# Token attention in a new order: values one pair behind, the compressed branch in spare score columns, outputs turned per pair, bias fetched sooner

## The chip, the cores and the metric

One NeuronCore of a Trainium2 chip runs the whole program in one launch. The metric is the device time in microseconds (us), the median of the runs shown. The engines are called by what they are: TensorE (PE in the profile, PEld its weight loads), VectorE (DVE), ScalarE (ACT), GpSimd (POOL) and SyncE (SP, which issues the loads of weight tiles).

## The reference

x is 256 tokens by 1024 features. Four mixers and their feed-forward layers follow each other: latent attention, an mLSTM, a short convolution, and last a token attention with three branches ("nsa"). Only the last matters here. It has 16 heads of 64 in 4 key groups:

```
proj = x @ w_q                                   # 1024 query columns, 48 gate columns
q    = rmsnorm per head(proj[:, :1024])
gate = sigmoid(proj[:, 1024:])                   # (head, branch)
s_c  = q @ k_c.T / 8 + bias                      # 15 compressed keys
o_c  = softmax(s_c) @ v_c                        # zero for the first 31 tokens
s_s  = q @ k_s.T / 8 + bias; o_s = softmax(s_s) @ v_s     # all 256 keys, causal
s_w  = q @ k_w.T / 8 + bias; o_w = softmax(s_w) @ v_w     # all 256 keys, causal
out  = (gate0 * o_c + gate1 * o_s + gate2 * o_w) @ w_o
```

With 256 tokens both the selected and the window branch see every earlier key, so a head has two score matrices of the same shape and the same bias, with other keys and values. The bias depends on the distance between query and key through 32 buckets.

## The kernel before

**Weights.** 522 tiles of 128 x 1024 float32 stream through four slots (`raw`). SyncE loads a slot when the tile before it has been split. ScalarE copies the tile to a rounded form (`split`, L502 to L510, `w_hi`), VectorE takes the rest (`take_lo`, L960, `w_lo`), GpSimd does this (L446) for tiles in three stretches, the last of them the tiles loaded during the query projection. A product is three matmuls of rounded operands, so most of the program is TensorE fed by this stream. Order on each engine is the order of the text; engines meet through counting semaphores.

**Around the change.** `residual("out_2")` is the second half of the feed-forward layer before: 8 outputs of 3 tiles each. After it ScalarE issues eight DMAs (L936 to L941), 256 KB each, which lay the bias of every head out by query and key (`bias`, from `bias_dram`). `bias` shares its memory with `os`, which the feed-forward layer read.

`nsa` on TensorE (L1961) first projects the gates (one tile) and the queries (`token_major("nq")`, 8 tiles, 16 chunks, two halves of 8 heads). Pieces of the attention stand between chunks: turning the queries of the first half (L1964) after chunk 9, compressed scores (L1975) after 11, turning the compressed probabilities (L1986) after 13, compressed values (L1993) after 15. Compressed scores need the turned queries, which ScalarE copies out (L822) after squares, root and two splits. Then the second half of the compressed branch is done, and then the head loop:

- TensorE `scores` (L2005, L2006): per head and branch, 128 queries against 128 keys and 128 against 256. The operand is a copy of the head's queries with zeros in the other 64 rows, made by ScalarE (`queries`, L845).
- VectorE `logits` (L1507): scores times the query's norm plus bias, two instructions for both branches; `maxima` (L1515 to L1517): maximum per query and branch, negated.
- ScalarE `exps` (L853): four exponentials with accumulated sums.
- VectorE `scales` (L1522, L1526): gate over sum. GpSimd (L496) multiplies the probabilities by it.
- TensorE `turn_probs` (L2019): six 128 x 128 turns; ScalarE copies them (L861).
- TensorE `values` (L2034): both branches accumulate into one output; VectorE adds it to the compressed output (`outputs`, L1535).

Logits run two heads ahead, and the buffers of logits and probabilities are two each. After the last head the outputs are turned (L1804), split by ScalarE and VectorE into `os` (L694, L1158), and the output projection `residual_one("wo_n")` begins, with the other turns between its first chunks.

Of the kernel before, what the change touches and what calls it, by code (L numbers as in the profile page):

```python
# [27 lines left out]
ALU = mybir.AluOpType  # L28
# [108 lines left out]
def build(nc, x_in, tiles, vecs, rows, consts, rel_bias, w1c_k, w1c_v, w2c_k, w2c_v, y_out):  # L137
    ctx = ExitStack()
    with ctx:
# [31 lines left out]
        vtok = sb("vtok", [P, TB * 2 * G * DH])  # L171
        kcT = sb("kcT", [P, G * NC])
        vc = sb("vc", [G * NC, G * DH])

        with nc.sbuf_tensor("os", [P, KD * 2 * S], F32R) as os_:
            pass
# [16 lines left out]
        def const(name, a, z, p=slice(None)):  # L193
# [39 lines left out]
        n_gturn, n_sqd, n_sum, n_std_, n_turn, n_qTd, n_cs, n_clog, n_cexp, n_cT, n_cTs, n_cpv, n_co = (  # L233
            sem(f"n_{n}") for n in ("gturn", "sqd", "sum", "std", "turn", "qTd", "cs", "clog", "cexp", "cT", "cTs", "cpv", "co"))
        n_gs, n_pg = sem("n_gs"), sem("n_pg")
        n_zero = sem("n_zero")
        n_q, n_s, n_log, n_max, n_exp, n_pT, n_pTd, n_pv, n_od = (
            sem(f"n_{n}") for n in ("q", "s", "log", "max", "exp", "pT", "pTd", "pv", "od"))
# [128 lines left out]
        n_qT = [[part(14720 + S * (2 * j + e), S) for e in range(2)] for j in range(2)]  # L367
        n_l = [part(8896 + 768 * j, 768) for j in range(2)]
        n_p = [part(10432 + 768 * j, 768) for j in range(2)]
        n_pTs = [part(11968 + 768 * j, 768) for j in range(2)]  # L370
        n_mx, n_nmx, n_rs, n_sc = ([part(13504 + 16 * j + 4 * w, 4) for w in range(4)] for j in range(4))
        n_cl = [part(13568 + H * NC * tb, H * NC) for tb in range(TB)]
        n_cmx, n_crs, n_csc = (part(14048 + TB * H * j, TB * H) for j in range(3))
        n_cpT = arena[0:G * NC, 14144:14144 + 2 * S]
# [22 lines left out]
        SQ0 = {"mix_0": 0, "cq": KD} | {name: KD + 1 + KD * j for j, name in enumerate(RES)}  # L397

# [40 lines left out]
        def _(pool):  # L439
# [49 lines left out]
            for t in range(*POOL_TILES[2]):  # L489
                take_lo(t % RING, t)  # L490
            with pool.Fori(0, HG) as i:
                for w in range(4):
                    pool.wait_ge(n_gs, i * 4 + (w + 1))
                    for tb, (a, z) in enumerate([(0, P), (P, 3 * P)]):
                        probs = n_p[w % 2].rearrange("p (b c) -> p b c", b=2)[:, :, a:z]
                        ins = pool.tensor_tensor(probs, probs, n_sc[w][:, 2 * tb:2 * tb + 2].unsqueeze(2).to_broadcast([P, 2, z - a]), ALU.mult)  # L496
                    ins.then_inc(n_pg, 1)
# [3 lines left out]
        def _(act):  # L501
# [41 lines left out]
            def residual(name, per, outs=KD):  # L543
# [19 lines left out]
                if last:  # L563
                    for i in range(outs // 4):
                        four(i)
                else:
                    act.preload_act_table(ACT.Sqrt)
                    with act.Fori(0, outs // 4) as i:
                        four(i)
# [120 lines left out]
            def out_hi(name, chunks=range(KD), gain=None):  # L690

                for k in chunks:
                    act.wait_ge(o_turn[name], k + 1)
                    act.activation(hi_part(os_, k), bank(5 + k % 3, 0, S), ACT.Copy,  # L694
# [97 lines left out]
            def nsa():  # L792
# [3 lines left out]
                split(t0 + RING)  # L796
                act.wait_ge(n_zero, 1)
                act.wait_ge(n_gturn, 1)
                for tb in range(TB):
                    ins = act.activation(n_gate[:, tb * 3 * H:(tb + 1) * 3 * H], bank(7, tb * 3 * H, (tb + 1) * 3 * H), ACT.Sigmoid,  # L800
                                         scale=rstd[:, tb:tb + 1])
                ins.then_inc(n_gates, 1)
                for t in range(t0 + 1, t0 + 4):
                    split(t + RING)

                def squares(g):
                    act.wait_ge(out_read, OUT0["nq"] + 2 * g + 2)
                    if g:
                        act.wait_ge(n_sum, 2)
                    for tb in range(TB):  # L810
# [71 lines left out]
                def four(i):  # L882

                    last = isinstance(i, int) and i == HG - 1
                    for w in range(4):
                        if w % 2 == 0 and not last:
                            queries(i + 1, w // 2)
# [1321 lines left out]
```

## Time and profile before

| what | us |
|---|---|
| median of 3 runs | 1666.72 (1665.49 to 1666.77) |
| the profiled run, its own time | 1666.71 |
| its span | 1664.9 |
| TensorE busy | 1602.7 |
| VectorE, ScalarE, GpSimd busy | 1099.6, 885.4, 163.7 |
| first matmul of the query projection | 1334.39 |
| first matmul of the output projection | 1452.53 |

Times inside the profile count from the start of the span. A row of a timeline gives the start, the duration, the engine, the line and the shapes, xN where N alike instructions are merged, and in brackets how long the engine was idle before it and what ended the wait. A matmul's duration includes its way through the array, so the next one starts before it ends: the distance of starts is what it costs. A float32 matmul appears as two instructions.

### The profile page before, as it was taken

Reading aid. Unit: us, or ns where it says so; the run is one execution under the profiler, and the core shown is the slowest. Engines: PE = TensorE matmul, PEld = TensorE weight load, DVE = VectorE, ACT = ScalarE, POOL = GpSimd, SP = SyncE. Lnnn points to the kernel's source line nnn. Section 1 sums busy time; section 2 is a strip of 40 time slices with the busy share of each in tenths; the row PEclk is TensorE's granted clock in tenths of the full one; section 3 lists DMA queues with packets and bytes.
Section 4 is the critical chain, followed back from the end, with each engine's and each line's share of the span. In section 5 each row is a group of like instructions: output and inputs, shape, how many; then the busy total and the mean of one; then the engine's idle time right before and its main releaser. Section 6 shows DMA issues by size and latency. Waiting matters only on the chain.

```text
span 1664.9 us, 33598 instructions
## 1 busy us (share of the span) xinstructions
PE 1602.7 (96%) x11652; PEld 1510.1 (91%) x11652; DVE 1099.6 (66%) x1770; ACT 885.4 (53%) x1468; POOL 163.7 (10%) x141
## 2 busy tenths in 40 slices
PE   7899999999999999999999999997999988799999
PEld 7789998977999899998999999897999867799997
DVE  6667766544876667667877666785566728676665
ACT  5676554535655445455446445544545546664443
POOL 1640000266000000000000000000000053300000
PEclk9999999989999999999999999998999989999999
DMA  6136566544566556556655555656455680055564
GB/s 228 64 82 199 188 190 190 176 131 135 178 190 188 191 176 198 182 187 203 191 188 189 190 188 187 206 182 196 145 189 186 210 171 15 1 175 186 184 197 142
DMA packets 81246, 282.81 MB, mean 170 GB/s; under 512 B 8848, under 2 KB 12432, under 8 KB 81168
## 3 DMA queue, kind: packets, MB, share of 16 engines
q1 hardware_dynamic: 77376, 276.88, 52.4%
q10 hardware_dynamic: 3792, 4.85, 1.7%
q8 instruction: 54, 0.88, 0.2%
q14 instruction: 24, 0.20, 0.0%
HBM read 280.12 MB, written 1.57 MB: 169 GB/s over the span
## 4 chain that ended last, share of the span: by engine, by line
PE 88%; DVE 5%; ACT 3%; issue 2%; DMA 1%; ACTq 1%; POOL 0%; DVEq 0%; SPq 0%; POOLq 0%
PE psum L1651 17%; PE psum L1653 17%; PE psum L1652 17%; PE psum L1643 17%; PE psum L1644 9%; PE psum L1779 2%; PE psum L1780 2%; PE psum L1781 2%; ACT arena L853 1%; DMA raw<-tiles 1%; DVE w_lo L968 1%; PE psum L2034 1%; PE psum L1941 1%; DVE arena L1517 0%; DVE arena L1516 0%
## 5 line engine op out<-in xcount | busy, mean ns | idle before, releaser
L510 ACT ACTIVATE w_hi<-raw 128x1024 fp32r<-128x1024 f32 x522 | 550.5, 1056 | 462.8 <-PE psum L1653 266.3
L968 DVE TENSOR_TENSOR w_lo<-raw,w_hi 128x1024 fp32r<-128x1024 f32 x476 | 582.0, 1223 | 229.0 <-ACT w_hi L510 228.2
L1651 PE MATMUL psum<-xs,w_hi 128*128 128x256 f32 x1960 | 550.7, 281 | 6.1 <-DVE w_lo L968 5.0
L1653 PE MATMUL psum<-xs,w_lo 128*128 128x256 f32 x1960 | 549.8, 280 | 0.0
L1652 PE MATMUL psum<-xs,w_hi 128*128 128x256 f32 x1960 | 547.9, 280 | 0.0
L1643 PE MATMUL psum<-hs,w_hi 128*128 128x512 f32 x1216 | 421.9, 390 | 0.0
L1651 PEld LDWEIGHTS psum<-xs,w_hi 128*128 128x128 f32 x1960 | 369.6, 189 | 7.2 <-DVE w_lo L968 5.5
L1652 PEld LDWEIGHTS psum<-xs,w_hi 128*128 128x128 f32 x1960 | 369.7, 189 | 0.2
L1653 PEld LDWEIGHTS psum<-xs,w_lo 128*128 128x128 f32 x1960 | 369.2, 188 | 0.0
L1644 PE MATMUL psum<-hs,w_lo 128*128 128x256 f32 x1216 | 343.4, 282 | 0.0
L1643 PEld LDWEIGHTS psum<-hs,w_hi 128*128 128x128 f32 x1216 | 228.3, 188 | 47.1
L448 POOL TENSOR_TENSOR w_lo<-raw,w_hi 128x1024 fp32r<-128x1024 f32 x46 | 110.3, 2411 | 1228.1 <-ACT w_hi L510 1198.0
L1644 PEld LDWEIGHTS psum<-hs,w_lo 128*128 128x128 f32 x1216 | 230.5, 190 | 0.0
L1651 PE MATMUL psum<-os,w_hi 128*128 128x256 f32 x544 | 154.5, 284 | 1.6 <-DVE os L1158 1.6
L1652 PE MATMUL psum<-os,w_hi 128*128 128x256 f32 x544 | 152.7, 281 | 0.0
L1653 PE MATMUL psum<-os,w_lo 128*128 128x256 f32 x544 | 152.6, 281 | 0.0
L1651 PEld LDWEIGHTS psum<-os,w_hi 128*128 128x128 f32 x544 | 103.2, 190 | 2.5 <-DVE os L1158 2.4
L1652 PEld LDWEIGHTS psum<-os,w_hi 128*128 128x128 f32 x544 | 103.2, 190 | 0.0
L1653 PEld LDWEIGHTS psum<-os,w_lo 128*128 128x128 f32 x544 | 103.1, 189 | 0.0
L991 DVE SCALAR_TENSOR_TENSOR xs<-x,vec,xs 128x256 fp32r<-128x256 f32 (+1 forms) x80 | 38.1, 482 | 51.7 <-ACT xs L524 51.7
L524 ACT ACTIVATE xs<-x,vec (+1 forms) x80 | 40.2, 509 | 54.3 <-DVE x L1058 31.2
L1106 DVE TENSOR_TENSOR fsum<-psum,sil 128x256 f32<-128x256 f32 x88 | 37.4, 425 | 46.0 <-PE psum L1653 44.7
(282 smaller groups left out, 1643.8 us busy)
## 6 DMA issues: line engine op xcount, KB each, us to landing
raw<-tiles SPq DMA_DIRECT2D x522, 512.0 KB, 4.2
bias<-bias_dram ACTq DMA_DIRECT2D x8, 256.0 KB, 12.5
x<-x_in SPq DMA_DIRECT2D x4, 256.0 KB, 5.7
y_out<-x SPq DMA_DIRECT2D x8, 128.0 KB, 3.5
con<-consts SPq DMA_DIRECT2D x1, 771.0 KB, 9.2
bias_dram<-bias_row ACTq DMA_DIRECT2D x1, 512.0 KB, 7.2
row<-rows SPq DMA_DIRECT2D x1, 192.0 KB, 9.2
vec<-vecs SPq DMA_DIRECT2D x1, 80.5 KB, 1.9
```

Of the source, the lines that this page charges most:

```text
L448: pool.tensor_tensor(w_lo[s][:, :], raw[s][:, :], w_hi[s][:, :].bitcast(F32), ALU.subtract).then_inc(lo_ready, 1)
L510: act.activation(w_hi[s][:, :], raw[s][:, :], ACT.Copy).then_inc(hi_ready, 1)
L524: act.activation(dst, src, ACT.Copy, scale=gain).then_inc(xhi_ready, 1)
L968: dve.tensor_tensor(w_lo[s][:, :], raw[s][:, :], hi_of(w_hi[s][:, :]), ALU.subtract).then_inc(lo_ready, 1)
L991: dve.scalar_tensor_tensor(out=dst, in0=src, scalar=gain, in1=hi_of(hi), op0=ALU.mult, op1=ALU.subtract).then_inc(xs_ready, 1)
L1106: dve.tensor_tensor(f, bank(b, 0, S), sil[u // 2][:, :] if u % 2 else rb[:, :], ALU.mult).then_inc(out_read, 1)
L1643: pe.matmul(bank(out_bank), w_hi[s][:, c:c + P], src[:, chunk:chunk + 2 * S], start=first, stop=False)
L1644: return pe.matmul(bank(out_bank, 0, S), w_lo[s][:, c:c + P], src[:, chunk:chunk + S], start=False, stop=last)
L1651: pe.matmul(out, w_hi[s][:, c:c + P], x_hi, start=first, stop=False)
L1652: pe.matmul(out, w_hi[s][:, c:c + P], x_lo, start=False, stop=False)
L1653: return pe.matmul(out, w_lo[s][:, c:c + P], x_hi, start=False, stop=last)
L1779: pe.matmul(out, x_hi, w_hi[s][:, col:col + 512], start=c == 0, stop=False)
```

## The change

- **Bias.** `residual("out_2")` is given `between=bias_rows` on ScalarE: DMA number g goes out after output g. The bias row is stored negated.
- **Queries.** They are evacuated with minus 1/8 of the norm's factor, normalised per head by VectorE before the turn, and the turn of the first half stands after chunk 13. Scores are thus negated logits, and minima take the place of maxima. `n_l` has four buffers, in the memory of `xs`.
- **Gates.** Sigmoid is computed as 1 / (1 + exp(-x)), beside the other exponentials.
- **Scores.** For a pair of heads at once, straight from the turned queries: head 0 of the pair in rows 0 to 63, head 1 in rows 64 to 127, alternately.
- **Logits.** `tensor_tensor_reduce`: bias added and the minimum taken in one instruction, four per head.
- **Values.** `vtok` has a column of ones per head, so the row sums come with the values. Branches have separate columns; VectorE scales them by gate over sum, GpSimd adds them and the compressed output. Values run one pair behind the turns.
- **Compressed branch.** Its scores, turns and values use columns 384 to 511 of the score banks, one step per pair, ahead of the pair's scores.
- **Outputs.** Output chunk k is turned when pair k is complete (`n_oo`), chunks 0 and 1 before the last turn of probabilities; banks by `out_bank`.
- All loops over heads are written out.

```diff
+            def bias_rows(g):
+                act.dma_start(bias[g * COPIES:(g + 1) * COPIES, :].rearrange("p (h s) -> p h s", h=H),
...
+            residual("out_2", FF2_TILES, between=bias_rows)
...
                 squares(0)
+                roots(0)
                 split(t0 + 4 + RING)
-                roots(0)
                 queries_turned(0)
                 split(t0 + 5 + RING)
+                squares(1)
+                roots(1)
+                act.preload_act_table(ACT.Exp)
+                exps(0, 0)
+                gates()
                 compressed_exps(0)
                 exps(0, 1)
+                for k in range(PAIRS):
+                    if k == 2:
+                        queries_turned(1)
+                    probs_turned(k, 0)
+                    if k + 1 < PAIRS:
+                        exps(k + 1, 0)
+                    probs_turned(k, 1)
+                    if k == 3:
+                        compressed_exps(1)
+                    if k + 1 < PAIRS:
+                        exps(k + 1, 1)
+                    if k < 2:
+                        split(t0 + 6 + k + RING)
...
+                def logits(k, e):
+                    h = 2 * k + e
+                    dve.wait_ge(n_s, h + 1)
+                    if k >= 2:
+                        dve.wait_ge(n_exp, h - 3)
                     for tb, (a, z) in enumerate([(0, P), (P, 3 * P)]):
+                        table = bias[:, h * S + (P if tb == 0 else 0):(h + 1) * S]
+                        for br in range(2):
+                            m = 2 * tb + br
+                            ins = dve.tensor_tensor_reduce(out=n_l[h % 4][:, br * 384 + a:br * 384 + z], in0=bank(n_bank[2 * e + br], a, z), in1=table,
+                                                           scale=1.0, scalar=3.0e38, op0=ALU.add, op1=ALU.min,
+                                                           accum_out=n_mn[h % 4][:, m:m + 1])
+                def outputs(k, e):
+                    dve.wait_ge(n_pv, h + 1)
+                    then(dve.reciprocal(ri.unsqueeze(2), pv[:, :, DH:DH + 1]))
+                    then(dve.tensor_tensor(sc..., ri..., gate4[:, :, h, 1:3], ALU.mult))
+                    dve.tensor_tensor(n_br[h % 4]..., pv[:, :, 0:DH], sc..., ALU.mult).then_inc(n_od, 1)
...
+                for k in range(PAIRS):                       # VectorE
+                    if k + 1 < PAIRS:
+                        logits(k + 1, 0)
+                        dve.wait_ge(n_s, 2 * k + 4)
+                        g, step = divmod(k + 1, 4)
+                        if step == 0:
+                            compressed_logits(g)
+                        if step == 1:
+                            compressed_turned(g)
+                        if step >= 2:
+                            compressed_outputs(g, step - 2)
+                    if k:
+                        outputs(k - 1, 0)
+                    if k + 1 < PAIRS:
+                        logits(k + 1, 1)
+                    if k:
+                        outputs(k - 1, 1)
+                    if k % 4 == 0:
+                        compressed_scales(k // 4)
...
+                def scores(k):                               # TensorE
+                    if k == PAIRS // 2:
+                        pe.wait_ge(n_qTd, 4)
+                    pe.wait_ge(n_log, 2 * k)
+                    g, step = divmod(k, 4)
+                    if step == 0:
+                        compressed_scores(g)
+                    if step == 1:
+                        compressed_turn(g)
+                    if step >= 2:
+                        compressed_values(g, step - 2)
+                    for block in BLOCKS:
+                        for e in range(2):
+                            ins = score(k, e, *block)
...
+                warm(12, 6)
+                for k in range(PAIRS):
+                    if k == 0:
+                        turn_probs(0, 0)
+                    if k + 1 < PAIRS:
+                        scores(k + 1)
+                    if k == 2:
+                        turn_queries(1)
+                        values(1, 0)
+                    if k:
+                        turn_probs(k, 0)
+                    if k not in (0, 2):
+                        values(k - 1, 0)
+                    if k == PAIRS - 1:
+                        pe.wait_ge(n_log, H)
+                        turn_outputs("o_n", no_tok, (n_oo, 1), range(2))
+                    if k == 2:
+                        values(1, 1)
+                    turn_probs(k, 1)
+                    if k not in (0, 2):
+                        values(k - 1, 1)
+                values(PAIRS - 1, 0)
+                values(PAIRS - 1, 1)
+                turn_outputs("o_n", no_tok, (n_oo, 1), range(2, 4))
```

## Rows read from the trace of the kernel before

**Rows 1.** The page: its first line, and from the list of DMA issues the weight tiles.

```profile
span 1664.9 us, 33598 instructions
...
raw<-tiles SPq DMA_DIRECT2D x522, 512.0 KB, 4.2
```

**Rows 2.** Busy time by stretches, start:end, length, then each engine; last clock, DMA share, GB/s.

```profile
1262.00:1331.00 69.00, 69.00 (x423) 62.15 (x422) 48.51 (x69) 37.96 (x53) 0.00 (x0) 1.00 0.63 199
1334.40:1352.80 18.40, 18.35 (x84) 14.38 (x83) 3.46 (x10) 6.25 (x9) 9.55 (x4) 1.00 1.11 173
1358.80:1372.30 13.50, 13.48 (x52) 11.12 (x52) 4.17 (x15) 7.08 (x13) 5.33 (x3) 0.71 0.31 95
1372.30:1388.40 16.10, 13.12 (x75) 11.00 (x75) 12.80 (x37) 11.17 (x31) 3.40 (x3) 0.89 0.18 63
1388.40:1451.00 62.60, 49.59 (x378) 46.01 (x378) 45.28 (x113) 42.35 (x153) 24.15 (x30) 1.00 0.00 1
```

**Rows 3.** Timeline of ScalarE at the start of the stage.

```profile
1331.76 4.11 ACTq L939 DMA_DIRECT2D bias<-bias_dram  x7
...
1352.61 1.06 ACT L510 ACTIVATE w_hi<-raw 128x1024 fp32r<-128x1024 f32 x1 [5.35 <-DMA raw<-tiles]
```

**Rows 4.** Timeline of TensorE in and after the query projection.

```profile
1336.57 0.40 PE L1779 MATMUL psum<-w_hi,xs 128*128 128x512 f32 x1
1336.81 0.40 PE L1780 MATMUL psum<-w_lo,xs 128*128 128x512 f32 x1
...
1358.82 3.62 PE L1975 MATMUL psum<-kcT,arena 128*128 128x30 f32 x16 [6.06 <-ACT arena L822]
...
1375.89 1.87 PE L1975 MATMUL psum<-kcT,arena 128*128 128x30 f32 x16
```

**Rows 5.** Timeline of TensorE in the head loop, and the output projection's first matmul.

```profile
1391.78 0.39 PE L2005 MATMUL psum<-kT,arena 128*128 128x128 f32 x2
...
1393.09 1.50 PE L2034 MATMUL psum<-vtok,arena 128*128 128x128 f32 x12
1394.43 0.82 PE L2019 MATMUL psum<-con,arena 128*128 128x128 f32 x6
...
1452.53 0.39 PE L1651 MATMUL psum<-os,w_hi 128*128 128x256 f32 x1 [0.50 <-DVE os L1158]
```

**Rows 6.** Timeline of VectorE between the projection and the head loop.

```profile
1370.60 1.41 DVE L1441 TENSOR_SCALAR arena<-psum,rstd 128x512 f32<-128x512 f32 x2 [4.55 <-PE psum L1781]
...
1377.31 0.17 DVE L1517 TENSOR_SCALAR arena<-arena 128x4 f32<-128x4 f32 x1
...
1377.88 0.41 DVE L1464 TENSOR_TENSOR arena<-psum,arena 128x56 f32<-128x56 f32 x2
...
1379.31 0.41 DVE L1476 TENSOR_TENSOR arena<-arena 128x56 f32<-128x56 f32 x2
```

**Rows 7.** Timeline of VectorE in the head loop.

```profile
1427.37 1.13 DVE L1507 SCALAR_TENSOR_TENSOR arena<-psum,arena,bias 128x256 f32<-128x256 f32 x2
...
1430.64 0.76 DVE L1517 TENSOR_SCALAR arena<-arena 128x4 f32<-128x4 f32 x1
...
1431.51 1.13 DVE L1507 SCALAR_TENSOR_TENSOR arena<-psum,arena,bias 128x256 f32<-128x256 f32 x2
```

**Rows 8.** Timeline of ScalarE in the head loop, one head.

```profile
1427.29 0.40 ACT L853 ACTIVATE arena<-arena 128x128 f32<-128x128 f32 x1 [1.44 <-DVE arena L1517]
1427.60 0.19 ACT L853 ACTIVATION_READ_ACCUMULATOR arena<-arena 128x1 f32 x1
...
1429.06 0.84 ACT L845 ACTIVATE arena<-arena 64x256 f32 x2
```

**Rows 9.** Timeline of GpSimd in the head loop.

```profile
1429.77 1.61 POOL L496 TENSOR_TENSOR arena<-arena 128x256 f32<-128x256 f32 x2 [2.54 <-DVE arena L1526]
```

**Rows 10.** DMA queues in 1325:1400, the queue of the bias; packets, MB, share.

```profile
q10 hardware_dynamic: 2176, 2.10, 20.6%
```

**Rows 11.** Timeline of ScalarE in the residual stage before.

```profile
1296.36 1.06 ACT L510 ACTIVATE w_hi<-raw 128x1024 fp32r<-128x1024 f32 x1 [1.59 <-PE psum L1644]
```

More of the change, by code:

```diff
@@ L541, in residual_one, with residual @@
                         split(t0 + u + RING, i)
-            def residual(name, per, outs=KD):
+            def residual(name, per, outs=KD, between=None):
                 t0, o0 = TILE0[name], OUT0[name]
@@ L882, in four @@
[L882 to L887, printed above, removed]
-                        probs_turned(i, w)
-                        if not (last and w >= 2):
-                            exps(i if w < 2 else i + 1, (w + 2) % 4)
-                four(0)
-                with act.Fori(1, HG - 1) as i:
-                    four(i)
@@ L1555, in nsa @@
+                logits(0, 1)
+                gates()
                 query_scales(1)
-                compressed_logits(1)
-                logits(0, 1)
-                maxima(0, 1)
-                compressed_scales(1)
-                scales(0, 0)
-                compressed_outputs(1)
-                dve.wait_ge(n_co, 2)
-                def four(i):
-                    first, last = (isinstance(i, int) and i == j for j in (0, HG - 1))
-                    for w in range(4):
-                        two_on = (i if w < 2 else i + 1, (w + 2) % 4)
-                        if not (last and w >= 2):
-                            logits(*two_on)
-                        if not (last and w == 3):
-                            scales(i if w < 3 else i + 1, (w + 1) % 4)
-                        if not (last and w >= 2):
-                            maxima(*two_on)
-                        if not (first and w == 0):
-                            outputs(i if w else i - 1, (w - 1) % 4)
@@ L1590, in _ @@
+                out_lo("o_n", range(2))
+                outputs(PAIRS - 1, 0)
+                outputs(PAIRS - 1, 1)
+                out_lo("o_n", range(2, KD))
             dve.wait_ge(vec_loaded, 16)
@@ L2048, in nsa @@
-                compressed_turn(1)
-                scores(0, 2)
-                compressed_values(1)
-                def four(i):
-                    first, last = (isinstance(i, int) and i == j for j in (0, HG - 1))
-                    for w in range(4):
-                        if not (last and w >= 1):
-                            scores(i if w < 1 else i + 1, (w + 3) % 4)
-                        if not (first and w == 0):
-                            values(i if w else i - 1, (w - 1) % 4)
-                        turn_probs(i, w)
@@ L2062, in nsa @@
[L2062 to L2067 removed]
+                                                  13: lambda: turn_queries(0)})
+                pe.wait_ge(n_qTd, 2)
+                for block in BLOCKS:
+                    ins = score(0, 0, *block)
+                ins.then_inc(n_s, 1)
+                pe.wait_ge(out_read, OUT0["nq"] + 4)
```

402 lines of the change are left out of this document (182 added, 220 removed).

## The prediction

> **What bounds the kernel now.** I read the page first, then the busy table by stretches, then the timelines of each engine inside the stretch that the change touches, since that is where a gap has an owner. In the weight-streaming stages TensorE has no gap: in 1262:1331 it is busy all 69 us at granted clock 1.00 while the DMA engines are 0.63 busy [rows 2]. The change leaves those stages as they are. It touches the token attention, from the query projection (first matmul at 1334.4, the start of its stretch in [rows 2]) to the first matmul of the output projection at 1452.53 [rows 5]: 118.1 us. There are three parts.
>
> First, the projection. One 512-column matmul starts 0.24 us after the last [rows 4]; 16 chunks of 6 matmuls, a gate turn of 0.4 and a query turn of 0.9 are 24 us, yet the stretch at the lower clock, which holds the last five chunks, reaches to 1372.3 [rows 2], and the second evacuation, which needs only the last chunk, starts at 1370.60 [rows 6]. TensorE stands 6.06 us before L1975 [rows 4]: that matmul waits for the turned queries, ScalarE copies them late, and ScalarE stood 5.35 us for a weight tile [rows 3]. The tile was late because ScalarE had issued seven bias DMAs from 1331.76 [rows 3] whose queue took 20.6% of 16 engines over 75 us, 15.5 us in all [rows 10]. After the gap the clock is down: 0.71 in 1358.8:1372.3 [rows 2].
>
> Second, 1372.3 to 1388.4: compressed branch of groups 8 to 15, between VectorE, ScalarE and TensorE by turns, clock 0.89 [rows 2].
>
> Third, the head loop, 1388.4 to 1451, TensorE busy 49.6 of 62.6 [rows 2]. One head is 4.15 us (from the start of L1507 at 1427.37 to its next at 1431.51, [rows 7]). No engine fills it; it is a ring: exponentials with their four accumulator reads, 1.77 us from 1427.29 to 1429.06 [rows 8], then the reciprocal, the gate product, two maxima and their negation on VectorE up to 1431.4 (L1517's end, [rows 7]), then the next exponentials. L1517 alone is 0.76 us for 4 columns, against 0.17 outside the loop [rows 6, 7]; in the loop it starts at 1430.64 under the POOL product that runs from 1429.77 for 1.61 [rows 7, 9], and it ends when that does. The Trainium skill has a rule for this (SBUF — State Buffer, Who interferes with whom, and the section before it on the two sides): whichever of GpSimd and a VectorE instruction in a two-port mode starts first keeps the pair, and the other "fully blocks". The trace agrees (0.76 against 0.17). By it the 0.6 us goes with L1517, and the new PSUM-reading instructions are not exposed.
>
> **The change, part by part.**
> *Bias fetched in the residual stage before.* The eight DMAs go out one per output of 7.6 us, behind the squares on ScalarE. Each takes 15.5/8 = 1.9 us of all engines, 0.25 of an output; with the 0.63 there [rows 2] that is 0.88. Cover: ScalarE splits a tile at 1296.36 [rows 11], VectorE has its rest 2.3 us later (two instructions of 1.06 and 1.2), and the slot is wanted again four tiles on, 4/3 of an output, 10.1 us; less 2.3, less 4.2 for the load [rows 1] leaves 3.6 us against 1.9. ScalarE pays 8 x 0.6 us of issue (4.11 for seven, [rows 3]) where it is 55% busy [rows 2]. I cost it at nothing; uncovered it is 8 x 1.9 = 15 us. The issues that stood before the norm's root vanish too, but nothing on TensorE's path waited for them.
> *Projection.* Queries are normalised before the turn, the turn moves to chunk 13, compressed scores, turns and values leave the projection. The chain to the turned queries starts with the first half, ready at 1334.4 + 11.6 = 1346.0: evacuation (two 512-column instructions, 1.4 by twice L1507's larger half), squares 0.6 after it, sums 0.7, root 0.3, reciprocal 0.3, two products 1.3: 1350.6, my estimate; the turn stands at 1354.3, so it is covered by over 3 us, and by 1 us if the short steps are double. Weight tiles: slots come free one per two chunks, 2.8 us, and each load is 4.2 us on four slots, so it is ready unless something else holds the queue. TensorE then ends the projection at 1334.4 + 16 x 6 x 0.234 + 1.3 = 1358.1, against 1370.5.
> *Start of attention.* In order from 1358.1: scores of head 0 1.3 (1391.78 to 1393.09 is one head, [rows 5]); second evacuation, until 1359.6; 8 compressed scores 1.9 [rows 4]; scores of head 1 1.3: 1362.9. VectorE: compressed logits 1.8 (from 1377.88 to the end of L1476 near 1379.7, [rows 6]), logits of head 1, 1.4: 1366.2. TensorE: the added 12 warm matmuls (2.6 us) lie under this, until 1365.5. Compressed turn 0.5, scores of pair 1 (1.9, below): 1368.7.
> *Scores from a pair of heads on row halves.* Now 1.31 us a head, 2.6 a pair. After, the same columns, but each matmul uses 64 rows and neighbours use different halves. No row shows two at once. Ends: 1.3 (all overlap) and 3.0 (none, and 0.2 lost at either end). The nearest row is L1975, 16 passes with 30 columns in 1.87 us [rows 4]: there the weight loads set the pace, and a pair's scores have 16 too. I take 1.9. Beside this, the Trainium skill says (TensorEngine Tiling (Array Packing), sections Key Properties and Theoretical Speedup) that 64-row tiles give up to 2x, but that a change of tiling mode drains TensorE, here twice per pair. By the first S would be 1.3; by the second alone, above 2.6. Both ends are in my range from the rows.
> *Logits fused with the minimum.* L1507 (2 instructions, 1.13, [rows 7]), the two maxima L1515 and L1516 and L1517 become 4 instructions of 128 or 256 columns. Low end: the L1507 time, 1.1. High end: L1507 plus both maxima, 2.1 (the maxima fill 1429.6 to 1430.64 before L1517). Four instructions instead of two add about 2 x 0.15; I take L = 1.4 a head, and ScalarE's accumulator reads (0.19 each, half of it beside the next exponential, [rows 8]) go.
> *Outputs.* Row sums come with the values (a ones column), so there is reciprocal 0.2, gate product 0.2 and a 256-column product 0.4: 0.8 a head, instead of L1535's 0.3 and POOL's 1.61 on probabilities [rows 9]. POOL's adds are off the path until the end.
> *The ring after.* Scores of pair k+2 reuse the banks of pair k+1, so they wait for both its logits. From the end of scores: TensorE turns probabilities 0.66 (L2019's 0.82 less the pipelined tail) and takes values 1.34 (1393.09 to 1394.43, [rows 5]), 2.1 with the hand-over; outputs 0.8; logits 1.4; hand-over 0.1; scores 1.9. One pair is 6.3 us. Other bounds: TensorE 1.9 + 2 x 2.0 = 5.9; VectorE 2 x 2.2 = 4.4; ScalarE, now busy 42.4 us for 16 heads [rows 2] or 5.3 for two, loses the reads and the query copies: 4.5. Now two heads take 8.3.
> *Compressed branch inside.* On the ring: four blocks of value matmuls 0.9 each, compressed scores 1.9, turn 0.5, second query turn 0.9 less slack 0.2, compressed logits 1.8 less the 0.5 wait it fills, scales 0.7 of their 1.1: 8.7. The rest fills the 0.6 us in which VectorE waits for values.
> *End.* From the end of the last scores TensorE has turns and values: 4 turns 2.6, 6 values 8.1, four output turns 0.9: 11.6 us, all others inside. The last adds of POOL (0.5 + 0.8) end near +13.5; its chunk is wanted at +15.
> *Sum.* 1368.7, first interval 5.4 (two logits 2.8, the turned compressed weights 0.6, hand-over, scores 1.9; no outputs yet), 5 x 6.3 = 31.5, 8.7, 11.6: 1425.9. In the first interval TensorE idles 2.8 us; after such a gap the clock fell (0.89 in 1372.3:1388.4, [rows 2]): +1.5. First output matmul at 1427.4 against 1452.5: 25 us less. The profiled run took 1666.71, and its span 1664.9 [rows 1]; the median shown is 1666.72, so nothing is to be shifted: **1641.7**.
>
> **Rivals.**
> (a) Row halves overlap fully, S = 1.3: ring 5.7 a pair, 7 x 0.6 less: 1637. For it: different banks and rows; against: the weight loads.
> (b) No overlap with drains, S = 3.0, or the fused instruction at its high end 2.1: ring 7.1 to 7.4; 7 x 0.8 to 1.1 more: 1647 to 1649. Both together 1655.
> (c) The bias DMAs are not covered: up to 15 more, 1657. Against: the 3.6 us above; the loads waited once in [rows 3] only with all eight at once.
> (d) Slower: TensorE's clock falls to 1.2 GHz and stays there through the loop, since it now waits in each pair and half its rows rest in the scores. Then TensorE is the bound, 2 x 5.9 = 11.8 us a pair: 7 x 5.5 = 38, and 9 more in the compressed parts and the end: 1689. It decides from a ring over 9.9 us a pair. Against: 1.00 in the present loop at 79% busy [rows 2], where the new one is above 90%.
> (e) The change does little, as the loop's ring is replaced by an equal one: only the start gains, 12 us: 1655.
>
> **How the numbers follow.** Mine 0.50, (a) 0.13, (b) 0.21, (c) 0.04, (d) 0.04, (e) 0.08. My case alone is 1637 to 1646 (each hand-over of 0.1 could be 0.2, two a pair, and the clock term 0 to 3). The range that leaves out 2 in 10 goes from 1633 to 1656. A difference under 0.2% (3.3 us) could not be told from none. Faster: all but (d) and a tail, 0.94; within 0.2%: 0.02; slower 0.04.
>
> **What would show it.** Right: no gap of TensorE in the projection, its last matmul near 1358; no DMA wait of ScalarE in the residual stage; scores of a pair in 1.9 us; pair to pair 6.3 us without the compressed branch; four fused instructions in 1.4 us; clock 1.00 in the loop; first output matmul near 1427. Wrong: half clock there, a gap of TensorE in the residual stage, or turned probabilities waiting for exponentials instead of scores for logits.

## The result, and the profile after

The changed kernel takes 1636.34 us (median of 1635.40, 1635.66, 1637.02 and 1637.50), the kernel before 1666.11 (1662.73 to 1666.77, four runs): 29.8 us less, ratio 0.983, 95% interval 0.981 to 0.984. Run again later, unchanged, it took 1636.40 (ratio 0.982 [0.980, 0.985]). Forecast were 1641.7 and 25 us less, with 1633 to 1656 as the range. The profiled execution took 1635.4.

The page: first line, TensorE's share, and the two kinds of DMA, against [rows 1] and [rows 10].

```profile
span 1633.4 us, 33428 instructions
...
PE 1593.6 (98%) x11692; PEld 1501.7 (92%) x11692; DVE 1082.1 (66%) x1822; ACT 866.6 (53%) x1380; POOL 151.3 (9%) x133
...
raw<-tiles SPq DMA_DIRECT2D x522, 512.0 KB, 4.3
bias<-bias_dram ACTq DMA_DIRECT2D x8, 256.0 KB, 6.1
```

Busy time by stretches, with the columns of [rows 2]: the projection, the matmuls on ones, the 8 us around the second pair, two pairs of the loop.

```profile
1331.07:1354.98 23.91, 23.91 (x109) 18.90 (x108) 5.82 (x14) 9.79 (x13) 15.43 (x7) 1.00 0.52 157
...
1360.00:1364.40 4.40, 4.40 (x26) 4.33 (x26) 4.04 (x18) 3.33 (x11) 0.00 (x0) 0.64 0.01 2
...
1367.90:1376.00 8.10, 5.93 (x40) 5.24 (x41) 4.61 (x27) 5.75 (x15) 2.35 (x1) 0.79 0.00 0
...
1394.40:1409.70 15.30, 15.21 (x138) 13.38 (x136) 10.45 (x52) 10.03 (x27) 5.04 (x9) 1.00 0.01 2
```

The gap of [rows 4] is gone: TensorE is busy all 23.91 us of the projection. In two pairs of the loop it idles 0.1 of 15.3 us, where it idled 13 of 62.6 before.

Timeline of TensorE, from the projection's last matmul to the second pair, then one pair of the loop and the output projection's first matmul (start, duration, idle time before in brackets). L1999 is the scores, L1993 the compressed values, L2101 the matmuls on ones, L2032 the turn of the probabilities, L2048 the values.

```profile
1354.65 0.40 PE L1783 MATMUL psum<-w_hi,xs 128*128 128x512 f32 x1
1354.98 1.57 PE L1999 MATMUL psum<-kT,arena 64*128 64x128 f32 x8
...
1360.08 4.41 PE L2101 MATMUL psum<-ones 128*128 128x128 f32 x24
1364.32 0.82 PE L2032 MATMUL psum<-con,arena 128*128 128x128 f32 x6
...
1365.51 1.58 PE L1999 MATMUL psum<-kT,arena 64*128 64x128 f32 x16
1367.02 0.88 PE L2032 MATMUL psum<-con,arena 128*128 128x128 f32 x6
1370.07 2.08 PE L1993 MATMUL psum<-vc,arena 128*128 128x128 f32 x8 [2.17 <-DVE arena L1531]
1372.08 2.22 PE L1999 MATMUL psum<-kT,arena 64*128 64x128 f32 x16
...
1401.35 1.58 PE L1999 MATMUL psum<-kT,arena 64*128 64x128 f32 x16
1402.86 0.87 PE L2032 MATMUL psum<-con,arena 128*128 128x128 f32 x6
1403.57 1.50 PE L2048 MATMUL psum<-vtok,arena 128*128 128x128 f32 x12
1404.91 0.82 PE L2032 MATMUL psum<-con,arena 128*128 128x128 f32 x6
1405.57 1.50 PE L2048 MATMUL psum<-vtok,arena 128*128 128x128 f32 x12
1407.11 1.16 PE L1993 MATMUL psum<-vc,arena 128*128 128x128 f32 x8
1408.20 0.49 PE L1999 MATMUL psum<-kT,arena 64*128 64x128 f32 x4
...
1421.22 0.37 PE L1653 MATMUL psum<-os,w_hi 128*128 128x256 f32 x1
```

VectorE in the same pair: the first of the first head's four fused instructions (L1531, adds and minimum), the compressed outputs (L1517), the first of the three instructions of outputs (L1542 to L1547), the first and third of the second head's four. It answers to [rows 7]. `w1c_all` is the memory of `xs`, in which the logits now lie.

```profile
1403.06 0.29 DVE L1531 CUSTOM_DVE_ANT_0 w1c_all<-psum,bias 128x128 f32<-128x128 f32 x1 [0.54 <-PE psum L1999]
...
1404.17 0.69 DVE L1517 TENSOR_TENSOR w1c_all<-psum,arena 128x512 f32<-128x512 f32 x1
1405.11 0.18 DVE L1542 RECIPROCAL arena<-psum 128x4 f32<-128x4 f32 x1 [0.25 <-PE psum L2048]
...
1405.87 0.28 DVE L1531 CUSTOM_DVE_ANT_0 w1c_all<-psum,bias 128x128 f32<-128x128 f32 x1
...
1406.63 0.42 DVE L1531 CUSTOM_DVE_ANT_0 w1c_all<-psum,bias 128x256 f32<-128x256 f32 x1
```

Read together they are the ring. From the end of the scores at 1402.86: turn 0.71, values 1.34 (start to start), hand-over 0.20, outputs 0.76 (1405.11 to 1405.87), the second head's logits 1.18 to 1407.05, hand-over 0.06, compressed values 1.09, scores 1.51: 6.85 a pair, 5.76 without the compressed values. TensorE's own work in a pair is 0.71 + 1.34 + 0.65 + 1.34 + 1.51 = 5.55 and 1.09: 0.2 us less than the ring. The profile shows no idle time for it, but 1405.57 to 1407.11 is 1.54 us where one head's values take 1.34: the wait is there. So two bounds lie 0.2 apart, and an engine that is busy 15.21 of 15.30 us is still not quite the one that sets the pace.

**Where the 31.5 us between the two spans are.** The stage, from the projection's first to the output projection's first matmul, took 118.1 us before [rows 2, 5] and takes 1421.22 - 1331.07 = 90.15: 28.0 less. Behind it the two are equal (212.4 and 212.2). Another 3.3 us are ahead of it, where the change touches nothing but the bias DMAs in the residual stage; e11 is about them.

### The profile page after: what moved, and what is told of

Read it like the earlier page. It is cut to its first block, busy times and chain, and to the rows that moved or that the text cites. A ratio compares the mean times of both kernels' runs of the same rounds, so it can differ in the third digit from the quotient of the medians.

```text
span 1633.4 us, 33428 instructions
## 1 busy us (share of the span) xinstructions
PE 1593.6 (98%) x11692; PEld 1501.7 (92%) x11692; DVE 1082.1 (66%) x1822; ACT 866.6 (53%) x1380; POOL 151.3 (9%) x133
## 4 chain that ended last, share of the span: by engine, by line
PE 92%; DVE 4%; ACT 2%; issue 1%; ACTq 1%; DMA 0%; DVEq 0%; SPq 0%
PE psum L1653 18%; PE psum L1655 18%; PE psum L1654 18%; PE psum L1645 17%; PE psum L1646 9%; PE psum L1781 2%; PE psum L1782 2%; PE psum L1783 2%; PE psum L2048 1%; PE psum L1999 1%; DVE w_lo L979 1%; PE psum L2032 1%; PE psum L1947 1%; PE psum L1852 0%; PE psum L1845 0%
## 5 line engine op out<-in xcount | busy, mean ns | idle before, releaser
L458 POOL TENSOR_TENSOR w_lo<-raw,w_hi 128x1024 fp32r<-128x1024 f32 x46 | 110.8, 2420 | 1232.3 <-ACT w_hi L534 1202.1
```

What stands on the lines that cost most here:

```text
L458: pool.tensor_tensor(w_lo[s][:, :], raw[s][:, :], w_hi[s][:, :].bitcast(F32), ALU.subtract).then_inc(lo_ready, 1)
```

## The experiments

From each trace three marks are used: the projection's first matmul, the first scores, and the output projection's first matmul. "Ones" is the time from the first matmul on ones to the first turn.

| kernel | median us | ratio to before [95%] | projection begins | to first scores | ones | first scores to output projection |
|---|---|---|---|---|---|---|
| changed | 1636.34 | 0.983 [0.981, 0.984] | 1331.07 | 23.91 | 4.24 | 66.24 |
| e12, changed again | 1636.40 | 0.982 [0.980, 0.985] | 1333.67 | 25.45 | 2.78 | 63.18 |
| e2, bias late | 1637.53 | 0.984 [0.981, 0.987] | 1332.19 | 26.79 | 2.78 | 63.18 |
| e3, scores by head | 1643.29 | 0.986 [0.983, 0.990] | 1333.81 | 23.91 | 4.42 | 73.61 |
| e4, no ones | 1636.46 | 0.983 [0.979, 0.986] | 1332.51 | 25.43 | - | 63.38 |
| e5, logits split | 1650.04 | 0.991 [0.990, 0.993] | 1332.49 | 23.92 | 4.38 | 78.48 |
| e6, values same pair | 1645.97 | 0.989 [0.986, 0.991] | 1330.70 | 23.89 | 4.22 | 76.09 |
| e7, values 65 | 1633.37 | 0.982 [0.980, 0.984] | 1331.03 | 23.91 | 2.78 | 62.84 |
| e8, weights later | 1628.51 | 0.977 [0.975, 0.979] | 1323.86 | 25.32 | 4.41 | 66.34 |
| e9, together | 1626.50 | 0.977 [0.974, 0.980] | 1324.30 | 23.89 | 1.13 | 64.32 |
| e10, values forward | 1636.48 | 0.982 [0.980, 0.984] | 1337.05 | 23.90 | 2.79 | 63.52 |

Single runs of one kernel differ by 2 to 6 us, so an effect under some 2 us is read from the marks and not from a median. Each row's marks come from one profiled execution.

**e12: the changed kernel again.** No edit.

> The changed kernel once more, unchanged, on the chip of the last runs. Expected: 1636 us within 2; the projection's first matmul between 1330.7 and 1333.8 us as in the runs so far, the stage from there to the first output matmul 87 to 91 us, by whether the granted clock falls in the matmuls on ones (4.2 to 4.4 us) or not (2.8 us).

Its last two columns are the reason for repeating: the same code takes 66.24 us in one execution and 63.18 in another. The matmuls on ones, in the same place with the same neighbours (the granted clock is the third number from the end):

```profile
1364.09:1366.87 2.78, 2.78 (x25) 2.78 (x25) 2.56 (x16) 2.03 (x8) 0.00 (x0) 1.00 0.01 3
```

At 1.00 they take 2.78 us, at 0.64 in the stretch shown above 4.24; the first 8 us behind them lose another 1.6 (compressed values 2.0 for 1.09, scores 2.15 for 1.51). It fell in five of the nine profiled executions that hold the 12 matmuls on ones, and what chooses them is not known. The same happens at the start of the projection: in e1, e4, e8 and e12 about 3 of its first us are at half clock, and the column "to first scores" has 25.3 to 25.5 for 23.9 in the last three; in the ten other traces the clock stays up there, although TensorE's waits just ahead (0.8 and 0.85 us) are the same in e12 and in the changed kernel's first execution. In e12:

```profile
1334.70:1337.50 2.80, 2.80 (x8) 2.12 (x8) 1.15 (x5) 0.35 (x1) 2.31 (x1) 0.50 0.79 158
```

Comparisons below are therefore made within one kind: 66.2 with low clock there, 63.2 without.

**e1: the bias fetch alone, on the kernel before.**

```diff
-            residual("out_2", FF2_TILES)
-            act.wait_ge(bias_out, 16)
-            act.wait_ge(tile_done, TILE0["out_2"])
-            for g in range(P // COPIES):
-                act.dma_start(bias[g * COPIES:...], ...)
+            residual("out_2", FF2_TILES, between=bias_rows)   # one DMA behind each output
```

> The kernel before with one part of the change alone: the 8 bias DMAs are issued one by one inside out_2. Theory (as in the forecast): the projection loses its gap and lasts 23.9 us from its first matmul as in the changed kernel, not 36; the loop behind it is the old one, so of the change's 29.8 us about 11 to 13 come, 1653 to 1656 us. Rival: the start of the old loop waits for something else (its zero fills, its queries' copies), and only the 6.1 us of TensorE's gap come: about 1660 us.

Measured 1654.44 against 1665.80, ratio 0.994 [0.992, 0.996]: 11.4 us, within the theory's 11 to 13. In its trace the 6.06 us in front of the compressed scores are gone. The stage there is 110.8 us, 7.4 less than before, or 8.9 without the 1.5 us that its first 24 projection matmuls took longer at the lower clock (7.3 for 5.8). The projection did not come down to the theory's 23.9 us: it takes 28.6, since the compressed scores and turns still stand inside it.

**e2: the changed kernel with the bias fetched late.** The same edit backwards.

> The changed kernel with this one part undone: the bias DMAs are issued behind out_2 again. Theory: the projection is again 12 us longer and everything behind it is moved by that, the ring stays at 6.86 us with and 5.8 us without compressed values: 1647 to 1650 us. Rival: part of the longer projection is hidden by the new order, in which logits need the bias first: 1641 to 1644 us.

Both were wrong: 1637.53, no difference that can be told. The weight tile is late again, 18.1 us behind the projection's first matmul against 18.2 in [rows 3] (timeline of ScalarE, the wait in brackets), but TensorE stands only 2.69 us.

```profile
1350.27 1.06 ACT L534 ACTIVATE w_hi<-raw 128x1024 fp32r<-128x1024 f32 x1 [7.82 <-DMA raw<-tiles]
```

The query turn on TensorE, behind it:

```profile
1355.17 1.09 PE L1969 MATMUL psum<-con,arena 128*128 128x128 f32 x8 [2.69 <-DVE arena L1477]
```

The projection is 2.9 us longer (26.79 against 23.91), and that is all. In the kernel before, the compressed branch stood inside the projection and needed the turned queries half way; now only the query turn does, at chunk 13. Issued late, the same 8 DMAs cost 9 to 11 us in the old order and 3 in the new one, by the marks; the medians of e2 and the changed kernel do not separate the 3.

**e3: scores head by head.**

```diff
-                    for block in BLOCKS:
-                        for e in range(2):
+                    for e in range(2):
+                        for block in BLOCKS:
                             ins = score(k, e, *block)
```

> The changed kernel with a pair's 16 score matmuls issued head by head, not in turns of the two halves of the array's rows. Theory A (TensorE binds the loop): the 16 take about 2.6 us as before the change, not 1.51, in each of 7 pairs, and nothing hides it: +7 to +8 us, 1643 to 1645 us. Theory B (the chain logits, exps, turn binds as I forecast): the first head's scores are now ready as early as before or earlier (1.3 us of 2.6), its logits start at once, and less than half of it shows: +0 to +3 us.

7.0 us slower by the medians. The 8 matmuls (16 instructions) take 2.27 us (next row 1412.22) instead of 1.51, and the pair 7.61 (from 1402.34) instead of 6.86:

```profile
1402.34 2.34 PE L1999 MATMUL psum<-kT,arena 64*128 64x128 f32 x16
...
1409.95 2.34 PE L1999 MATMUL psum<-kT,arena 64*128 64x128 f32 x16
1412.22 0.87 PE L2032 MATMUL psum<-con,arena 128*128 128x128 f32 x6
```

Taking turns between row halves saves 0.76 us, all of it on the path: 7 x 0.76 = 5.3, and 2 more where the clock stayed low for longer. It does not separate A from B: the ring holds the whole of the scores, since the turn is queued behind them on TensorE. My B had the path through the first head's logits, which was wrong.

**e4: no matmuls on ones.** `warm(12, 6)` is left out.

> The changed kernel without the 12 matmuls on ones ahead of the first turn of probabilities. In the changed kernel they ran from 1360.08 to 1364.32 us, the first head's exponentials were done at 1361.02. Theory A (they stand in the way): the first turn starts at about 1361.1 and the stage gets 2 to 3.3 us shorter, 1633 to 1634.5 us. Theory B (they hold the clock): without them the granted clock of the next 10 us falls to half, the scores of pair 1 take 3 us and not 1.5, and the stage gets 1 to 4 us longer, 1637 to 1640 us.

No change in the time (1636.46). Both theories hold a half. The turn starts 6.1 us after the first scores instead of 9.3 (7.8 in e12), and then runs at half clock:

```profile
1364.05 1.39 PE L2032 MATMUL psum<-con,arena 128*128 128x128 f32 x6 [1.05 <-ACT arena L869]
...
1366.57 2.10 PE L1999 MATMUL psum<-kT,arena 64*128 64x128 f32 x16
```

The rest of the stage is 63.38 us, e12's 63.18. So the clock can fall with the ones or without them; with 12 of them they stand in the way. One trace without them doesn't tell how often it falls there.

**e5: the fused logits parted.**

```diff
-    ins = dve.tensor_tensor_reduce(out=..., in0=bank(...), in1=table, op0=ALU.add, op1=ALU.min, accum_out=...)
+    ins = dve.tensor_tensor(..., bank(...), table, ALU.add)
...
+    then(ins)
+    for tb, (a, z) in enumerate([(0, P), (P, 3 * P)]):
+        ins = dve.tensor_reduce(n_mn[h % 4][:, 2 * tb:2 * tb + 2], log[:, :, a:z], AX_X, ALU.min)
```

> The changed kernel with each head's four fused add-and-minimum instructions (1.11 us) parted into four adds and two minimum reductions with a wait between, about 2.3 us by the changed kernel's 0.28 and 0.42 us and the old reductions. Theory A (TensorE binds, VectorE idles 1.5 to 3.4 us in each pair): 2.4 us more VectorE work in a pair uses up that idle time and shows with at most 1 us a pair, the stage gets 1 to 7 us longer: 1637 to 1643 us. Theory B (the forecast's chain through VectorE binds): each head's 1.2 us stands in the chain, 2.4 us in each of 7 pairs: +17 us, 1653 us.

13.7 us slower: more than A, less than B. A pair takes 8.46 us (1410.99 to 1419.45), 1.6 more:

```profile
1410.99 1.16 PE L1994 MATMUL psum<-vc,arena 128*128 128x128 f32 x8 [1.57 <-DVE arena L1534]
...
1419.45 1.16 PE L1994 MATMUL psum<-vc,arena 128*128 128x128 f32 x8 [1.65 <-DVE arena L1534]
```

VectorE, from the end of the scores near 1405.2 to 1410.9:

```profile
1405.30 1.15 DVE L1530 TENSOR_TENSOR w1c_all<-psum,bias 128x128 f32<-128x128 f32 x4 [1.48 <-PE psum L2000]
1406.49 1.01 DVE L1534 TENSOR_REDUCE arena<-w1c_all 128x2 f32<-128x256 f32 x2
...
1408.75 1.14 DVE L1530 TENSOR_TENSOR w1c_all<-psum,bias 128x128 f32<-128x128 f32 x4
1409.93 1.01 DVE L1534 TENSOR_REDUCE arena<-w1c_all 128x2 f32<-128x256 f32 x2
```

A head's logits cost 2.12 instead of 1.11. The ring of the changed kernel holds only the second head's, so it would be 7.9; but now VectorE's own row (logits 2.12, a compressed step 0.59, outputs 0.74, logits 2.11) with scores, compressed values and 0.2 of hand-overs is 8.4, and has become the ring. Of VectorE's idle time in the changed kernel only the wait for values in front of the first head's L1542 was spare room (0.25 us in the pair above, 0.25 to 0.57 in the others that have one); the rest is its wait for scores, which comes back in every pair. That VectorE took over rests on this sum (8.4 against 8.46 measured); no further run varies it.

**e6: values behind their own pair.** The order within pair k becomes scores of k+1, both turns of k, both values of k.

> The changed kernel with the values of a pair issued behind the same pair's turns, not one pair behind. Theory: TensorE waits in each pair for ScalarE's copies of the turned probabilities (0.87 us for a head, behind the 1.5 us of the next exponentials), 1.5 to 3 us a pair that nothing else fills: the ring goes from 5.8 to 7.3 to 8.8 us, +10 to +20 us, 1647 to 1657 us. Rival (the order of the values is worth little, the gain is the fused logits and the shorter scores): under 4 us.

9.6 us slower, just under the theory's range: a pair takes 8.66 us. TensorE waits for ScalarE's copies before the second turn, and for VectorE's outputs before each of the values:

```profile
1409.50 1.58 PE L1999 MATMUL psum<-kT,arena 64*128 64x128 f32 x16
...
1412.29 0.85 PE L2032 MATMUL psum<-con,arena 128*128 128x128 f32 x6 [0.40 <-ACT arena L879]
1413.90 1.58 PE L2048 MATMUL psum<-vtok,arena 128*128 128x128 f32 x12 [0.76 <-DVE arena L1547]
1415.76 1.58 PE L2048 MATMUL psum<-vtok,arena 128*128 128x128 f32 x12 [0.28 <-DVE arena L1547]
```

**e7: 65 columns in the values.** `vtok[:, first_v:first_v + DH + 1]` for `first_v + P`.

> The changed kernel with 65 columns in each matmul of values and not 128 (the 63 columns behind a head's values and its ones are not used). Theory A (they are bound by their columns): 1.34 us a head become 0.7 us, 8 us less in 16 heads, and since TensorE binds, 5 to 8 us less: 1629 to 1631 us. Theory B (they are bound by the loads of 128x128 weights, one behind each matmul): the same 1.34 us, 1636 us.

B, nearly: half the columns take 0.05 us less of 1.34 a head, so the columns do not set the pace. That the loads of the weights do fits the trace: they are busy in all 1.29 us of these values, and the compressed scores, with 30 columns and weights as large, take 0.113 us an instruction (16 in 1.80) against 0.112 here with 128 and 0.107 with 65. The row of one head (the next starts 1.29 after it):

```profile
1400.37 1.45 PE L2048 MATMUL psum<-vtok,arena 128*128 128x65 f32 x12
```

The median's 3 us are not from this: 62.84 stands against 63.18 of the changed kernel at the same clock.

**e10: values half a pair sooner.** In pair k now turn of the first head, values of the second head of k-1, turn of the second head, values of the first head of k.

> The changed kernel with one new order alone: the values of a pair's first head are issued behind the same pair's second turn (the first pair's into the idle time of 2.2 us ahead of the second pair's scores), the second head's behind the next pair's first turn. Theory A (TensorE binds the ring): no pair gets shorter, the 1.34 us taken into the idle time are all there is: the stage 1.3 us shorter, and with a clock that stays up there 2 to 3 us, median 1633 to 1635.5 us. Theory B (the chain through VectorE binds): nothing, or 1 to 3 us longer, since outputs stand ahead of the next logits sooner.

Nothing gained (1636.48; 63.52 against 63.18), theory B. The idle time of 2.17 us is filled with values and reappears: 0.84 in the same place, 1.47 one pair later, released by the same logits.

```profile
1374.46 1.16 PE L1993 MATMUL psum<-vc,arena 128*128 128x128 f32 x8 [0.84 <-DVE arena L1531]
...
1381.40 1.16 PE L1993 MATMUL psum<-vc,arena 128*128 128x128 f32 x8 [1.47 <-DVE arena L1531]
```

**e8 and e11: the compression's weights.** A stage before the change's, ScalarE issues four DMAs in a row. The second of them, timeline of ScalarE's queue, in the kernel before:

```profile
1124.97 5.30 ACTq L769 DMA_DIRECT2D w1c_all<-w1c_v  x1
```

The same of the changed kernel:

```profile
1124.30 3.06 ACTq L796 DMA_DIRECT2D w1c_all<-w1c_v  x1
```

Code and place are the same, the issues are not: 5.30 and 3.06 us, and the third takes 4.8 in both. ScalarE does nothing else meanwhile, the keys' root comes behind, and TensorE waits for the keys: 8.7 us before, 6.5 after. All eleven traces without the edit below fall in two kinds: 3.0 to 3.4 us and a wait of 6.5 to 6.7 in eight, 4.7 to 5.3 us and 7.9 to 8.7 in three (before, e10, and e12, which is the changed kernel itself). Both experiments put the DMAs behind that root:

```diff
-            glu("glu_2", {0: key_roots, 9: compressed_hidden, ...})
+            glu("glu_2", {0: key_roots, 1: lambda: hidden_weights(0), 2: lambda: hidden_weights(1),
+                          3: output_weights, 9: compressed_hidden, ...})
```

> The changed kernel with the DMAs of the compression's weights issued inside glu_2, behind the root of the key norms, one at a time, and not ahead of it. In the changed kernel ScalarE stood 8.5 us in their issue (1122.9 to 1132.7) and TensorE then idled 6.5 us for the keys. Theory: that gap goes, 4 to 7 us less: 1629 to 1632 us; and since both kernels' times differ from run to run by how long that issue takes (4.4 to 5.3 us for the first two), the spread gets smaller. Rival: the compression then waits for its weights, and the time stays within 2 us.

> The kernel before with the compression's weights fetched inside glu_2, as in e8. It tells whether the part of the difference that lies ahead of the stage (3.3 us between the two profiled executions) belongs to the change. Theory (it does not: it is how long the issue of those DMAs happened to take): the gain is that of e8, 7 to 8 us, 1657 to 1659 us, and the projection then begins at the same time in both kernels within 1 us (1326 us). Rival: the two kernels still differ there by about 3 us.

e8 takes 1628.51, 7.8 less than the changed kernel where 4 to 7 were expected; its runs did not lie closer together (1622.86 to 1629.76, the changed kernel's 1635.40 to 1637.50). TensorE's only wait in 1100:1180 is 0.6 us (line, released by, total, times, longest):

```profile
PE psum L1951 <- DMA arena<-w2c_v: 0.6, 1, 0.6
```

e11, on the kernel before, takes 1657.00 against 1665.24, 8.2 less, ratio 0.995 [0.993, 0.996], and its five runs lie within 2 us. The projection begins at 1324.33 in e11 and at 1323.86 and 1324.30 in e8 and e9 (not at 1326, as I had expected): old and new within 0.5 us. So the 3.3 us ahead of the stage are not the change's; 2.2 of them are the kind of that issue. The changed kernel's own two traces begin the projection 2.6 us apart. With the issue moved out of both, new against old is e8 against e11: 1628.51 against 1657.00, 28.5 us, from two rounds in which the kernel before agrees within 0.5 us (1664.81 and 1665.24). That is the cleanest figure for the change here.

**e9: four edits together.** e8, e10, e7 and `warm(4, 6)`.

> The changed kernel with four edits: the compression's weights fetched inside glu_2 (e8), the first head's values taken forward into TensorE's idle time ahead of the second pair's scores (all values half a pair sooner, e10), 4 matmuls on ones and not 12 ahead of the first turn, 65 columns in the values. Expected from the parts, if they add up: -7.8 (e8), -1.3 (values forward), -1.5 to -3 (the matmuls on ones ran 1.4 to 3 us longer than the first exponentials), -0.8 (65 columns: 0.05 us in each of 16 heads): 1622 to 1626 us. If the clock falls at the shorter run of ones, as it did without any, 1625 to 1628 us.

1626.50, in the second of the two expected ranges, the one for a falling clock, and the fastest median of the study, 9.8 us under the changed kernel; 2 us under e8, which their spreads (1623.7 to 1631.2, 1622.9 to 1629.8) don't separate. Its ones take 1.13 us and the first turn starts as early as in e4, but idle times of 0.67, 1.11 and 1.51 us follow, and behind the last of them the half clock:

```profile
1368.11 2.08 PE L1997 MATMUL psum<-vc,arena 128*128 128x128 f32 x8 [1.51 <-DVE arena L1535]
1370.11 2.23 PE L2003 MATMUL psum<-kT,arena 64*128 64x128 f32 x16
```

The parts don't add up: e8 carries it, the other three are worth 0 to 2 us together.

## Why the prediction was right, by its steps

- **Projection.** Forecast 23.7 us to the first scores, measured 23.91. No gap, and none in the residual stage: in 1262:1327.7 TensorE is busy all 65.70 us with the DMA engines 0.82 busy, forecast 0.88. The cover of 3.6 us was enough; the DMAs land in 6.1 us, where they took 12.5 before. But the price of the parts was wrong where I did not separate them: of the 12.1 us, 8.9 belong to the bias in the old order (e1), the rest to the compressed steps that left; and with the new order the early fetch is worth only 2.9 (e2). The two parts overlap.
- **Start.** The second pair's scores end 35.95 us after the projection's first matmul, forecast 34.3. The ones took 4.24 us, where I had planned 2.6 and had them hidden under VectorE's logits until 1365.5. In e12 they took 2.78, so most of this term is the clock.
- **Scores on row halves.** 1.51 us a pair, forecast 1.9, between rival (a)'s 1.3 and mine; e3 gives 2.27 for the same matmuls without turns. The two changes of tiling in a pair cost little: a record overlaps the next by 0.16 us elsewhere in the loop (1404.91 + 0.82 over 1405.57) and by 0.07 at either end of the scores, and the turn behind them takes 0.71 where the other takes 0.65. By these rows a pair loses some 0.2 us at them, an estimate, since the ends of matmuls are modelled. The Trainium skill's "Up to 2×" (TensorEngine Tiling (Array Packing), Theoretical Speedup) is 1.74x here against the full-height matmuls of before (2.62 a pair), 1.50x against e3.
- **Fused logits.** 1.11 us a head and 0.07 for the last read of the accumulator, forecast 1.4. The bounds were 1.1 and 2.1. My 2 x 0.15 for two more instructions was too much: the first head's four start 0.21, 0.21 and 0.35 us apart.
- **Outputs.** 0.76, forecast 0.8.
- **Ring.** Forecast 6.3 without compressed steps, measured 5.76. The ring is the forecast's: scores, turn, values, outputs, logits of one head, scores. Its terms: scores -0.39, logits -0.22, outputs -0.04, turn and hand-overs +0.11. TensorE's own bound was given as 5.9, with 1.9 for the scores; with 1.51 it is 5.55.
- **Compressed steps on the ring.** 4 x 1.09 + 1.80 + 0.93 + 0.55 = 7.6, forecast 8.7: the compressed logits stayed off it.
- **Clock after the first idle time.** +1.55, forecast +1.5, in the execution that shows it; 0 in e12.
- **End.** From the last scores to the output projection 11.5, forecast 11.6.

From the second pair's scores to the last the sum had 47.1 us and the trace has 42.7: first interval -0.8, five rings -2.6, compressed steps -1.1. With the start's +1.65 the stage came 2.9 us shorter than forecast: errors of both signs; in e12's execution (88.63 us) it is 4.4 shorter. The mechanism was right, and the terms mis-sized were the scores and the logits. What carries it is not the one number: e3 puts the scores on the path with all they take, e10 shows that filled idle time comes back, and e5 and e6 lengthen the ring. Not undone by themselves in any run are the compressed branch in the spare columns, the turn of the outputs per pair and the new gates, so their shares are not known. The 3.3 us ahead of the stage also count in the comparison of the two profiled executions (28.0 and 3.3); they were no part of the sum, and e11 shows that they are no part of the change.

Of the rivals, (b), (c) and (e) are out: scores and logits at their low ends, no gap in the residual stage, a shorter loop. (d) did not happen: granted clock 1.00 in the loop. (a)'s 1637 lies nearest to the measured 1636.34, and that is partly luck: its scores of 1.3 are short of the 1.51, everything else was as I had it, and 3.3 us that belong to neither came on top.

The wait for GpSimd went as forecast with the old kernel's L1517 and its four columns. L1511, a product of two operands in SBUF, still takes 0.59 us at 1401.93, under GpSimd's addition of 0.72 from 1401.77, and 0.17 at 1370.86; the four fused ones, with one operand in PSUM, take the same 1.11 alone (from 1403.06) and beside a GpSimd addition of 0.45 at 1406.03 (from 1405.87). By the Trainium skill (SBUF — State Buffer, Who interferes with whom) an instruction of VectorE with two inputs in SBUF contends with GpSimd's reads, and one with at most one SBUF input, outside the two-port modes, does not; the trace agrees with both.

What stays open: what decides in which executions the clock falls in the first 10 us of the attention and in the first 3 of the projection, and how much of e1's 11.4 us is the difference between executions (its stage shows 7.4 to 8.9).

## What to carry to other kernels

Sum a ring link by link, with each engine's own sum beside it: here they lay 0.2 us apart, so that filled idle time came back a pair later (e10), and VectorE, 68% busy in the loop, had only some 0.25 to 0.57 us of spare room a pair, so that 2 us more made it the bound (e5). An edit has no price of its own: the early fetch was worth 9 to 11 us in the old order and 3 in the new. And an engine that issues DMAs can stand for microseconds in the issue itself, so put them behind the instruction that others wait for (8 us, e8 and e11; no further edit of the loop gave more than 3 by its median).

## What the hardware showed beyond this

- An issue of a DMA of many small rows took ScalarE 0.85 us as the first of a row and 3.0 to 5.3 us directly behind another of the same kind, in the same code; the third, of only 64 KB, took 4.7 to 4.9. Four in a row held ScalarE idle for 8.5 us in the changed kernel and 10.8 in the one before. Issued one per weight tile (e8) the first two took 0.85 and 1.13, the third still 3.44.
- Eight fp32 score matmuls (16 instructions) of 64 rows, 128 and 256 columns, take 1.51 us in turns of the row halves and 2.27 head by head; of 128 rows, before the change, 2.62.
- Six fp32 matmuls (12 instructions) on 128x128 weights take 1.34 us with 128 columns and 1.29 with 65.
- The granted clock fell within a stretch in which TensorE was busy without a gap (the ones, 0.50 in 1360:1363, behind 28.9 us without one) in some executions and not in others of the same kernel.
